# First expert pair's tokens found by rank and gathered whole by products; last output block spread in full precision

## The reference, cut to what matters

```
h2  = modulate(rms_norm(x, g_norm2), mod[3], mod[4])
aff = softmax(h2 @ w_router)                    # 512 tokens x 16 experts
g, idx = top_k(aff.T, 64)                       # each expert its 64 tokens
xs = h2[idx]
y  = (silu(xs @ w_gate) * (xs @ w_up)) @ w_down * g      # 2048 -> 1024 -> 2048
x  = x + mod[5] * scatter_add(y, idx)
```

## Time and profile before

| What | Value |
|---|---|
| median of three runs | 1987.07 us |
| profiled execution | 1986.9 us |
| its span | 1984.8 us |
| PE, DVE, ACT, POOL busy | 96%, 44%, 23%, 10% of the span |
| HBM read | 583.8 MB |
| granted TensorE clock, mean | 0.995 |
| last stage (experts) | from 1067.36 us, when the first piece's products begin |
| last weights taken up by PE | 1971.48 us |

### The profile page before, as it was taken

How to read it: one execution, slowest core, us unless ns; L and a number is a source line. 1 busy time by engine, 2 the same in 40 slices (tenths; PEclk the granted TensorE clock), 3 DMA queues, 4 the chain that set the end, 5 groups by cost and what they waited for, 6 DMA issues and landing times.

```text
span 1984.8 us, 26339 instructions
## 1 busy us (share of the span) xinstructions
PE 1905.8 (96%) x10396; PEld 1227.2 (62%) x10396; DVE 867.5 (44%) x1773; ACT 457.7 (23%) x1213; POOL 204.2 (10%) x434
## 2 busy tenths in 40 slices
PE   4999999999999999999999999999989999998998
PEld 2578888888889989888876333535344353534433
DVE  5568878772256666644434130302213031221343
ACT  4233323222156666632222000000000000000000
POOL 0003112101145543100000000000000000000000
PEclk9999999999999999999999999999999999999999
DMA  9967988883112112242269999999999999999998
GB/s 402 421 237 278 345 313 287 294 286 135 41 57 91 47 46 83 106 170 106 106 249 375 430 421 430 432 431 430 431 432 432 431 428 431 430 431 433 430 424 358
DMA packets 69154, 602.29 MB, mean 303 GB/s; under 512 B 6685, under 2 KB 24349, under 8 KB 35113
## 3 DMA queue, kind: packets, MB, share of 16 engines
q1 hardware_dynamic: 55440, 589.01, 73.1%
q10 hardware_dynamic: 13160, 10.03, 1.5%
q0 software_dynamic: 432, 1.57, 0.2%
HBM read 583.80 MB, written 16.79 MB: 303 GB/s over the span
## 4 chain that ended last, share of the span: by engine, by line
PE 59%; DMA 9%; DVE 2%; ACT 1%; issue 1%; ACTq 0%; DVEq 0%
PE SM L1299 9%; PE TM L1299 8%; DMA arena<-in_w_twos 7%; PE TM L1342 5%; PE SM L1342 5%; PE TR L1246 2%; PE MJ L1246 2%; PE TM L1051 2%; DMA arena<-in_w_last 2%; PE MJ L926 2%; PE SM L1016 1%; PE SN L1286 1%; PE TN L1055 1%; PE TM L1077 1%; PE SM L1077 1%; PE TM L1079 1%
## 5 line engine op out<-in xcount | busy, mean ns | idle before, releaser
L1299 PE MATMUL SM<-arena 128*64 128x512 f32 x1024 | 249.9, 608 | 25.8 <-DMA arena<-in_w_twos 25.8
L1299 PE MATMUL TM<-arena 128*64 128x512 f32 x1024 | 244.0, 596 | 0.0
L1952 DVE SCALAR_TENSOR_TENSOR arena<-arena,csil 128x512 f32<-128x512 f32 x240 | 180.3, 751 | 13.0 <-DMA arena<-in_w_mod 3.0
L1299 PEld LDWEIGHTS SM<-arena 128*64 128x64 f32 x1024 | 71.6, 138 | 160.9 <-issue 159.2
L1299 PEld LDWEIGHTS TM<-arena 128*64 128x64 f32 x1024 | 77.5, 139 | 146.5 <-issue 146.5
L1342 PE MATMUL TM<-arena,cst 128*64 128x512 f32 x512 | 116.9, 598 | 0.4
L1342 PE MATMUL SM<-arena,cst 128*64 128x512 f32 x512 | 115.9, 600 | 0.8 <-DMA arena<-in_w_last 0.7
L1652 ACT CAST y_hi<-arena 128x512 fp32r<-128x512 f32 x32 | 19.8, 618 | 379.7 <-DVE arena L2292 342.8
L1406 ACT ACTIVATE wh<-wr 128x1024 fp32r<-128x1024 f32 (+3 forms) x59 | 62.4, 1083 | 187.6 <-PE TN L830 137.8
L1861 DVE TENSOR_TENSOR wl<-wr,wh 128x1024 fp32r<-128x1024 f32 (+3 forms) x59 | 74.5, 1264 | 69.9 <-ACT wh L1406 69.8
L2247 DVE TENSOR_TENSOR brow<-cst,rope_t 128x512 f32<-128x512 f32 x8 | 5.5, 692 | 214.4 <-PE MJ L1272 214.3
(11 more groups left out here) (412 smaller groups left out, 3659.1 us busy)
## 6 DMA issues: line engine op xcount, KB each, us to landing
arena<-in_w_twos SPq DMA_DIRECT2D x68, 4096.0 KB, 22.6
arena<-in_w_mod SPq DMA_DIRECT2D x96, 1024.0 KB, 7.0
arena<-in_w_first SPq DMA_DIRECT2D x41, 2048.0 KB, 12.3
arena<-in_w_last SPq DMA_DIRECT2D x15, 2048.0 KB, 26.5
wr<-in_w_na SPq DMA_DIRECT2D x24, 1024.0 KB, 6.9
wor<-in_w_out SPq DMA_DIRECT2D x8, 2048.0 KB, 8.1
xT<-in_tokens_t SPq DMA_DIRECT2D x4, 1536.0 KB, 13.1
arena<-in_w_qkv SPq DMA_DIRECT2D x8, 640.0 KB, 5.3
```

The lines of the kernel that those rows point to most:

```text
L1299: mm = pe.matmul(GU[b][64 * e:64 * e + CAP, :], xsT[:, k, 64 * e:64 * e + CAP], w[:, 2 * (b // 2) + e, (b % 2) * NB:(b % 2 + 1) * NB], sta ...
L1952: ve.scalar_tensor_tensor(acc, row, c, acc, ALU.mult, ALU.add).then_inc(mod_step, 1)
```

## The change: what it does

1. **Ranks for the first pair.** Right after each tile's reciprocal DVE makes `lead_p`, the affinities of experts 0 and 1 times 2^60. PE spreads each over all partitions (`spread_lead`, two transposes a tile, L1203 of the changed kernel). DVE then compares, for each of the 8 combinations of tile and expert, 512 affinities with those of its 128 tokens in one instruction with a sum at the end (L2267); a constant `lead_mask`, 1 MB loaded once, breaks ties. Ranks below 64 are picked, PE counts them with the triangular matrix (`count_lead`), and `member` for the first pair follows. The eight rounds for all experts and what hangs on them come after that, between the copies of the first pair's blocks; the slot numbers for the other pairs, and the index for `rows_1`, come later too (`find_rows` after k = 7).
2. **All 16 blocks by products.** `rows_0`, its fetch, its scaling and its index are gone; `gather_first` uses four products for every k.
3. **ACT scales x1 by blocks of 512 columns**, 16 instructions in place of 4.
4. **Last block in full precision.** `spread_last` makes one float32 product a token tile from `y_sb` into four different PSUM banks; the split of that block is gone.
5. `keep_clock` counts change: 5 and 48 in place of 4, 7 and 56; the one between turning and counting goes.

```diff
-            keep_clock(4)
+            spread_lead(0)
+            spread_lead(1)
             turn_aff(LT - 2)
-            keep_clock(7)
+            spread_lead(2)
+            keep_clock(5)
+            spread_lead(3)
             turn_aff(LT - 1)
-            keep_clock(56)
+            keep_clock(48)
+            count_lead()
             keep_clock(4)
...
-                if k >= KD // 2:
-                    if k == KD // 2:
-                        pe.wait_ge(rows_set, 1)
-                    at = (k - KD // 2) * P
-                    pe.transpose((TR, MJ)[k % 2][:, 0:P], rows_0[:, at:at + P], ident[:]).then_inc(xt2_full, 1)
-                    return
...
+            def spread_last():
+                pe.wait_ge(y_done, 4 * PAIRS)
+                for tile in range(LT):
+                    if tile >= 2:
+                        pe.wait_ge(acc_done, 16 * (PAIRS - 1) + LT * (MODB - 2) + tile + 1)
+                    pe.matmul(LAST_SUM[tile], memberT[:, tile * P:(tile + 1) * P].bitcast(F32), y_sb[(MODB - 1) % 2],
+                              start=True, stop=True).then_inc(add_full, 1)
...
                     gate_up(pair, k)
                     if pair == 0 and k + 2 < KD:
                         gather_first(k + 2)
-                    if pair == 0 and k in (0, 2):
-                        find_rows(k // 2)
+                    if pair == 0 and k == 5:
+                        turn_picked()
+                    if pair == 0 and k == 6:
+                        count_picked()
+                    if pair == 0 and k == 7:
+                        find_rows()
...
-            for tile in range(LT):
-                sc.wait_ge(e_rsd, 2 * tile + 1)
-                sc.activation(x1[:, tile, :], x1[:, tile, :], ACT.Copy, scale=e_rs[:, tile:tile + 1]).then_inc(x1_scaled, 1)
-            sc.wait_ge(rows_0_in, 16)
-            sc.activation(rows_0, rows_0, ACT.Copy, scale=rows_rs[0]).then_inc(rows_set, 1)
+            sc.wait_ge(e_rsd, 2 * LT)
+            for nb in range(MODB):
+                cols = slice(nb * NB, (nb + 1) * NB)
+                for tile in range(LT):
+                    sc.activation(x1[:, tile, cols], x1[:, tile, cols], ACT.Copy, scale=e_rs[:, tile:tile + 1]).then_inc(x1_scaled, 1)
...
+                    ve.scalar_tensor_tensor(junk_lead[n % 2], LEAD[e], lead_p[:, tile, e:e + 1], lead_mask[:, tile, :], ALU.subtract, ALU.is_gt,
+                                            accum_out=lead_rank[:, tile, e:e + 1]).then_inc(few_set, 1)
...
+            for k in range(3, 6):
+                take_first(k)
+                top_eight(2 * k - 4)
+                top_eight(2 * k - 3)
```

More of the change, by code:

```diff
@@ L433, in build_layer @@
         tri = arena.take(159 * K, P)
+        lead_mask = arena.take(148 * K, LT, SEQ)
+        junk_lead = [arena.take((144 + 2 * i) * K, SEQ) for i in range(2)]
         cst = sb("cst", [P, CONSTS + 2 * KD * 2 + UNITS * HEADS])
@@ L1185, in _, with spread_lead, count_lead @@
                     turn_aff(tile - 2)
+            def spread_lead(tile):
+                pe.wait_ge(few_set, LEAD_FROM + tile + 1)
+                if tile == 0:
+                    pe.wait_ge(y_free, LT * 2 * MODB)
+                for e in range(2):
+                    mm = pe.transpose(LEAD[e][:, tile * P:(tile + 1) * P], lead_p[:, tile, e:e + 1].broadcast_to([P, P]), ident[:])
+                mm.then_inc(few_full, 1)
+            def count_lead():
+                pe.wait_ge(few_set, RANKED + 1)
+                flat = lead_t.rearrange("p a b -> p (a b)")
+                for i in range(LT):
+                    mm = pe.matmul(SN[:, 2 * i:2 * LT], ones[:] if i else tri[:], flat[:, 0:2 * (LT - i)], start=(i == 0), stop=(i == LT - 1))
+                mm.then_inc(few_full, 1)
@@ new lines, in turn_picked, with count_picked @@
+            def turn_picked():
+                pe.wait_ge(few_set, REST_FROM + 1)
+                for tile in range(LT):
+                    mm = pe.transpose(SN[:, tile * N_EXP:(tile + 1) * N_EXP], picked[:, tile * P:(tile + 1) * P], ident[0:N_EXP, 0:N_EXP])
+                mm.then_inc(few_full, 1)
+            def count_picked():
+                pe.wait_ge(few_set, REST_FROM + 2)
+                flat = picked_t[:].rearrange("p a b -> p (a b)")
+                for i in range(LT):
+                    mm = pe.matmul(TN[:, i * N_EXP:LT * N_EXP], ones[:] if i else tri[:], flat[:, 0:(LT - i) * N_EXP],
+                                   start=(i == 0), stop=(i == LT - 1))
+                mm.then_inc(few_full, 1)
@@ L1248, in gather, with find_rows @@
                 mm.then_inc(xt2_full, 1)
[L1250 to L1254, removed]
+            def find_rows():
+                pe.wait_ge(member_set, 2)
+                pe.wait_ge(idx_set, 1)
                 for tile in range(LT):
-                    mm = pe.matmul(SN[:, 0:2], (member, member_1)[pair][:, tile, :], token_no[:, tile, :], start=(tile == 0), stop=(tile == LT - 1))
+                    mm = pe.matmul(SN[:, 0:2], member_1[:, tile, :], token_no[:, tile, :], start=(tile == 0), stop=(tile == LT - 1))
                 mm.then_inc(idx_full, 1)
@@ L1658, in _ @@
                     sc.wait_ge(rows_1_in, 32)
[L1659 removed]
+                    sc.activation(rows_1, rows_1, ACT.Copy, scale=rows_rs).then_inc(rows_set, 1)
                 if pair == PAIRS - 1:
@@ L2168, in soft_end @@
                 ve.wait_ge(lg_rec, tile + 1)
+                ve.tensor_scalar(lead_p[:, tile, :], probs_r[:, tile, 0:2], r_inv[:, one], 2.0 ** 60, ALU.mult, ALU.mult).then_inc(few_set, 1)
+                ve.wait_ge(few_set, LEAD_FROM + tile + 1)
                 ve.tensor_scalar(p, p, r_inv[:, one], None, ALU.mult).then_inc(lg_aff, 1)
@@ L2386, in _ @@
                 accumulate(pair, 2, 2, LT)
-                low_rows(pair, 3)
+                if more:
+                    low_rows(pair, 3)
             accumulate(PAIRS - 1, 3, 0, LT)
```

122 lines of the change are left out of this document (78 added, 44 removed).

## The result

| | before | changed |
|---|---|---|
| median, us (range, runs) | 1986.56 (1985.87 to 1987.30, 20) | 1989.47 (1987.71 to 1992.01, 20) |
| ratio, 95% interval | | 1.0016, 1.0010 to 1.0022 |
| profiled execution: time, span | 1986.9, 1984.8 | 1992.01, 1990.2 |
| a second profiled execution of the changed kernel | | 1989.35, 1987.5 |

The account below looks back on a forecast made before the run. The weight stream was taken to bound the kernel, held by PE at the first pair's down pieces. Stream +2.7 and tail -0.95 gave +1.75 on 1986.9, 1988.65, stated as 1988.7; own range 1986.8 to 1990.8, wider range 1985.0 to 1991.5.

Parts of the forecast that it names:

- Start: Router's end: PE's 48 constant products, not DVE's ranks, set the start; piece 0 begins at 1063.95, 3.4 us earlier.
- The rule of halved throughput: DVE comparisons: two non-bf16 SBUF sources halve throughput; taken literally, the sum would be 1.6 us more.
- rival C: Slower: comparisons take 1.5 us and down pieces show full landings, 1991.4; DVE copies waiting behind rounds, 1996. Chance 0.2.
- PE within the pair: First pair: gather products, turning and counting add 7.2 us on PE; last gate piece ends 3.8 us later, at 1139.3.
- The stream: Weight stream from the first pair's down pieces on: held by PE's later return of slots, +2.7 us.
- the lead of 0.9: At 1153.3 the stream is 0.9 us ahead of PE's returning of slots, read from landings of 9.1 against 8.2.
- The hole at 1068: Gap in the weight stream before piece 10, 4.0 us; shrinks to about 0.6 us as piece 10 is issued earlier.
- The landing: Landing of a 2 MB weight piece without a queue: 8.2 us read, 6.8 us estimated by the skill's formula.
- The tail: Kernel's end, y_sb to last add: four full-precision products in place of split and pairs, -0.95 us.
- A: Rival: the hole closes and PE does not hold the stream; 5.6 us won, 1981.4. Chance 0.08.
- B: Rival: piece 0 begins as early as x1's scaling allows, 1059.3, or PE's steps are shorter; 1985.1. Chance 0.14.
- D: Rival: the tail stays the same because the last adds wait on DVE; 1989.6, within the forecast's range.

Follow-up runs that it names:

- The seventeen products without any gather: Kernel before the change plus 17 constant products on PE after piece 10 of the first pair (3.85 us); 1989.38 us, ratio 1.0015.
- tail only: Kernel before the change with only the last output block in full precision; 1985.21 us, ratio 0.9994.
- 17 products and the new tail: Kernel before the change plus 17 constant products after piece 10 of the first pair and the full-precision last block; 1988.17 us, ratio 1.0009.
- the cheap gather: Changed kernel with one transpose of x1 for each of blocks 8 to 15, without picking tokens, so not computing the layer; 1983.71 us, ratio 0.9987.
- the kernel that fetches: Changed kernel with first-pair blocks 8 to 15 again fetched and transposed, and 26 constant products in place of 48; 1981.68 us, ratio 0.9976.
- the 26 products: Changed kernel with 26 in place of 48 products on constants ahead of the count; 1986.46 us, ratio 1.0000.
- unused fetch: Changed kernel with the first pair's fetch, row numbers, copies and scaling put back but its rows not used; 1989.76 us, ratio 1.0018.

## Why the prediction was right, and where not

The forecast of 1988.7 us, its range of 1985.0 to 1991.5 and "no change" held; the measured 1989.47 lies 0.8 above it. In differences the miss is larger: +1.75 was forecast on a profiled execution of 1986.9, and +2.9 was measured on a median of 1986.56. By its steps:

- *Start.* Piece 0 was forecast at 1063.95 and began at 1064.03; last gate piece 1139.3, measured 1139.14. The second execution had 1064.48 and 1139.59. The comparisons took 0.67 us each instead of 0.83, so the ranks stood 4.9 us before the end of PE's constant products (1060.2) and not 3.8. That gained nothing, since the products were later anyway. That they hold the start was right: taking 22 away gave 3.0 us.
- *The rule of halved throughput.* The comparison took 0.75 and 0.71 to 0.73 us, with a source in PSUM and a mask in SBUF, so rival C falls in its first half. What the Trainium skill, "Vector Engine (DVE) Microarchitecture Reference", section 7, says is of two non-bf16 SBUF sources. The comparison is not that case and does not test it; the row that speaks against it is the 0.751 us of two SBUF sources beside 0.750 with one in PSUM, both without a sum.
- *PE within the pair.* Forecast +3.8 at the last gate piece, measured +3.65 and +4.1. The forecast took it for granted that the down pieces come later by as much, but the piece issued at 1153.3 before came 3.7 and 2.5 us later: in the second execution the clock did not fall at 1140 us, as it had in the trace of before. The terms stand in the chain: 0.35 for turning, 0.80 for counting, 0.79 for one find_rows, 1.09 a block. The seventeen products without any gather reproduce this lateness (last gate piece +3.7).
- *The stream.* Forecast +2.7, measured +2.72 in the typical execution. In the slowest one the last landing comes 4.6 us later, and it is taken up 5.4 us later. That PE holds the stream from 1153 on is borne out, but the match to a few hundredths is luck. By the forecast's rule, lateness less the lead of 0.9, the two executions would have given 2.5 - 0.9 = 1.6 and 3.7 - 0.9 = 2.8. Measured are 1.1 and 1.8 more, which come with the restart, for which the forecast had no term. In the second execution the clock that stayed up took back 1.6 of PE's lateness (4.1 at the last gate piece, 2.5 at this issue), so the two misses cancel. The lead itself rests on one landing of 8.2 us. In the traces pieces that found the queue empty or nearly so landed after 7.4 to 8.8 us, so that the lead could be read as anything from 0.3 to 1.7. The expected landings of 8 to 9 us from 1157 on did not come: after 7.9 and 7.8 us the next ones took 10.3 and 10.0. By its words that touches the forecast's own sign of being wrong, landings near 1160 above 10 us. It does not mean that PE had a lead there, since each of these stands right behind one that found the queue empty.
- *The holes.* The hole at 1068 was forecast at 0.6 us and kept 6 x (1 - 317/432) = 1.6. What I did not see is that it does not close but moves. Piece 10 is issued earlier, so piece 16 has landed at 1107.5, while piece 17 can't be issued before PE is done with piece 8, at 1107.0. The next run dry comes at 1152. That is the second half of rival C, in a mild form. The executions of the changed kernel range over 4.3 us, those of before over 1.4. The range is 2.4 to 4.3 us in the five kernels that run dry at about 1150 (with 11 or more runs), 1.1 in the one without any hole, but 3.2 and 3.3 in two without a clear hole there. The clock may do as much: the 1.2 us by which the two executions differ at the down pieces would reach the end once PE holds the stream. Which of the two makes the range is not shown.
- *The landing.* The Trainium skill, "DMA: Bandwidth & Descriptors", section "Anatomy of one DMA", gives its formula for transfers issued by GpSimd, and the weights are issued from SP, so the estimate of 6.8 us in the prediction was worked out for another path. 7.9 us in the first execution and 8.2 us before are measured.
- *The tail.* Forecast -0.95, measured 4.49 for 5.42, -0.93. This step was right in kind and size.
- **The step that was mis-sized:** what lies behind the last add was taken over at 3.45 us without a term of its own. It measured 4.35 and 4.37, +0.9 in the span. With the 0.3 us that the new end saves outside the span it is +0.65 in the time, and that is nearly all of the 0.7 between the forecast's +1.75 and the +2.45 of the profiled executions. Of the +0.9 some 0.2 to 0.4 come with the shorter tail (3.67 in "tail only", 3.84 with 17 products and the new tail). That the output's transfers, 256 KB each, then follow those of the block before without a pause and queue is the likely reason, not a shown one. Another 0.5 to 0.6 comes when the fetch is dropped with what belongs to it (3.79 when it is put back). All four traces without the fetch have 4.35 to 4.49, all five with it and the new tail 3.67 to 3.84. It is also a part of the 2 us by which the expectation for the cheap gather fell short, while that of the kernel that fetches (1981.6 for 1981.68) did not. It can't explain the 26 products, whose expectation started from the changed kernel. The other 0.46 of the 2.9 us between the medians is that the profiled execution of before was 0.34 above its median and the second one of the changed kernel 0.12 below.
- *Rivals.* A falls, the stream was held by PE. B falls, the products did stand in PE's order and piece 0 began no earlier than 1064.0. D falls: the tail is shorter, though most of it is given back behind it.

Open stays why so little of the DMA engines is left at work at the end when 128 half rows (144 of the 432 packets in the software queue, below) are not fetched some 900 us earlier. The medians of the tail's two comparisons (-1.3 and -1.2 us, each uncertain by some 1.8) are larger than the 1.0 and 0.7 that the traces and the time outside the span give, which the noise allows. The queue of the two pages, changed kernel and unused fetch:

```profile
q0 software_dynamic: 288, 1.05, 0.2%
```

```profile
q0 software_dynamic: 432, 1.57, 0.2%
```

## What to carry to other kernels

Look for the place where the stream has its thinnest lead over the engine that returns its buffers, and judge each part of a change there. A small lead need not be a gift: here 0.9 us were read, and none of them was left once the stream had run dry and restarted. Ranks and tail won 3.0 us with the 48 products on constants and 4.9 with 26, and the 6.6 us of gather products took back 6.0. Give the output behind the last operation a term of its own, count what lies outside the span, and take a second profile when the first is at the edge of its runs. Compare the granted clock of the two before comparing anything else.

## What the runs showed of the hardware

After the stream of the changed kernel has run dry at 1152, the DMA share returns to 0.94 to 1.00 within a few microseconds while GB/s stay at 350 to 393 in place of 430 (windows from 1158 and 1164 us), and landings come 6.6 to 8.0 us apart twice in both executions before they fall back to 4.9 (with one more of 6.4 in the first). The same kernel, with the same wait of 1.16 us on PE at 1140 us, had a granted clock of 0.73 from 1140 to 1146 in one execution and 1.00 in another. A comparison with its sum lets the next one start after 0.67 us, with the reading of the sum (0.07) overlapping it; the form without a sum did the same (start at 1977.91, next operation at 1978.58, duration 0.75), so its duration overstates what it costs in a row. And the kernel with a fetch of 0.5 MB at 1070 us, unused, ended otherwise at 1985 than the one without: 219 and 21 GB/s in the same 0.6 us before the end.
